# Decoder trunk on one core: 48 of the 64 chunk products of the recurrent output projection moved into the last three rounds as plain fp32

## What is computed

```python
def rwkv7_time_mix(...):
    ...
    y = rwkv7_scan(rh, decay.reshape(B, S, H, N), kh, vh, -kk, kk * ah)
    ...                                   # per-head norm, bonus
    out = ((y + bonus.reshape(B, S, D)) * g).astype(h.dtype) @ w_o
    return out, v_first

x = x + y
x = x + swiglu_ffn(rms_norm(x, ffn_norm[layer]), ffn_w_in[layer], ffn_w_out[layer])
```

## Time and profile before

| | us |
|---|---|
| time, median of 3 runs (1957.79 to 1961.66) | 1959.42 |
| the profiled execution: its own time | 1955.48 |
| the profiled execution: span from first to last instruction | 1953.7 |
| round 3, gated to gated (sixteen projection products) | 52.45 |
| round 4 (sixteen) | 52.93 |
| round 5 (eight) | 52.42 |
| round 6 (none) | 50.61 |
| round 7 (none, and no "after" part) | 35.62 |
| round 8 (none, only the "before" part) to the first `w_o` product | 20.54 |
| first `w_o` product to the end of the first feed-forward tile | 51.28 |

### The profile page before, as it was taken

One profiled execution on the slowest core, in us unless ns is written; L12 is line 12 of the kernel. 1 busy time (PEld: TensorE's weight loads), 2 busy tenths in 40 slices (PEclk: granted clock), 3 DMA queues, 4 the chain that ended last, 5 costly groups with the idle time before them and its releaser, 6 DMA issues.

```text
span 1953.7 us, 35112 instructions
## 1 busy us (share of the span) xinstructions
PE 1853.1 (95%) x15020; PEld 1425.4 (73%) x15020; DVE 946.0 (48%) x1593; ACT 781.8 (40%) x1326; POOL 205.1 (10%) x174
## 2 busy tenths in 40 slices
PE   8978999987889999999999999999999799999999
PEld 3745666655658888888887877777777588888887
DVE  6624555555535444443355545545554564444422
ACT  4333343333324222222345656566656442222211
POOL 0032333323210000000011111111111000000000
PEclk9989999998879999999999999999999899999999
DMA  3281010100213333333332222222222133333332
GB/s 119 78 262 35 17 30 29 29 27 5 70 37 94 100 95 99 95 105 91 95 99 85 69 73 76 85 68 76 76 69 72 30 101 97 97 97 97 97 97 97
DMA packets 57539, 154.95 MB, mean 79 GB/s; under 512 B 5591, under 2 KB 22535, under 8 KB 57384
## 3 DMA queue, kind: packets, MB, share of 16 engines
q1 hardware_dynamic: 57288, 152.63, 25.8%
q10 hardware_dynamic: 96, 0.07, 0.0%
HBM read 150.51 MB, written 11.61 MB: 83 GB/s over the span
## 4 chain that ended last, share of the span: by engine, by line
PE 86%; ACT 4%; DVE 4%; issue 3%; SPq 1%; DMA 1%; POOL 0%; ACTq 0%; DVEq 0%
PE bank L500 84%; PE bank L503 2%; ACT f L1415 2%; ACT f L1428 1%; SPq L459 1%; DMA f<-stream 1%; DVE f L1628 1%; SPq L442 1%; DVE f L1636 0%; ACT f L1402 0%; ACT f L1174 0%; DVE f L1511 0%; DVE f L1514 0%; DVE r L1488 0%; DVE f L1595 0%
## 5 line engine op out<-in xcount | busy, mean ns | idle before, releaser
L500 PE MATMUL bank<-r 128*128 128x512 f32 x5616 | 1304.8, 392 | 7.0 <-DVE r L1915 3.7
L500 PEld LDWEIGHTS bank<-r 128*128 128x128 f32 x5616 | 1051.0, 188 | 241.9 <-issue 18.0
L500 PE MATMUL bank<-f 64*64 64x64 f32 (+3 forms) x8940 | 503.8, 258 | 70.0 <-DVE f L1605 12.4
L500 PEld LDWEIGHTS bank<-f 64*64 64x64 f32 (+2 forms) x8940 | 321.1, 143 | 234.2 <-issue 120.9
L1488 DVE TENSOR_TENSOR r<-f,r 128x1024 fp32r<-128x1024 f32 x230 | 283.0, 1231 | 390.4 <-ACT r L1102 390.4
L1102 ACT ACTIVATE r<-f 128x1024 fp32r<-128x1024 f32 x230 | 240.7, 1047 | 153.4 <-PE bank L500 138.2
L2066 POOL TENSOR_TENSOR r<-f,r 128x512 fp32r<-128x512 f32 x48 | 62.2, 1297 | 886.1 <-ACT r L1393 886.1
L1372 ACT ACTIVATE r<-f 128x512 fp32r<-128x512 f32 x44 | 27.8, 632 | 218.1 <-DVE f L1808 218.1
L1839 DVE TENSOR_TENSOR f<-bank,f 128x512 f32<-128x512 f32 x72 | 56.0, 777 | 87.6 <-PE bank L500 84.6
L503 PEld LDWEIGHTS bank<-f 128*128 128x128 f32 x464 | 54.3, 143 | 48.6 <-ACT f L1428 26.9
L503 PE MATMUL bank<-f 128*128 128x128 f32 x464 | 70.4, 282 | 20.3 <-ACT f L1428 14.3
(11 more groups left out here) (110 smaller groups left out, 974.6 us busy)
## 6 DMA issues: line engine op xcount, KB each, us to landing
f<-stream SPq DMA_DIRECT2D x247, 512.0 KB, 3.6
bias_copies<-bias_rows SPq DMA_DIRECT2D x3, 3072.0 KB, 25.5
f<-xT SPq DMA_DIRECT2D x16, 256.0 KB, 4.1
f<-lora_out SPq DMA_DIRECT2D x16, 128.0 KB, 3.9
f<-bias_copies SPq DMA_DIRECT2D x16, 128.0 KB, 3.3
f<-bias_copies SPq DMA_DIRECT2D x32, 64.0 KB, 3.0
outT<-f SPq DMA_DIRECT2D x8, 256.0 KB, 4.5
f<-const SPq DMA_DIRECT2D x1, 576.0 KB, 3.9
```

Source lines behind the costliest of these rows:

```text
L500: return nc.tensor.matmul(out, lhsT, rhs, start=start, stop=stop, skip_group_check=True)
```

## The change

Of the 64 (tile, chunk) products of the output projection, 48 are computed while the rounds still run, as plain fp32 products like those of `project`, in the places where `project` has nothing left to do: 15 in round 6, 16 in round 7 and 17 in round 8. They take the tiles in turn: five chunks of tiles 0, 1 and 2, six of tiles 3 and 4, seven of tiles 5, 6 and 7. All sum up in bank 6, tile 6 in bank 5. DVE adds each partial tile to x (`partial(m)`), and PE waits for that before it begins the next tile in the bank. The other sixteen products are plain fp32 too, from two panels of their own (`wo_last`), in banks 2, 3 and 4: six stand right behind the last round, ten behind the last pair's output. The first two feed-forward tiles are computed together, chunk by chunk (`first_pair`), between and behind the last of these products, and `norm_sum` follows both. The six `w_o` panels of the early products are no longer split, nor are the time mixer's outputs, and so `output_high`, `output_low` and the splits of `w_o` panels go. In all three `residual` calls the scaled copy (a `tensor_scalar` on DVE) goes: ACT rounds straight from x with the gain as scale, and DVE forms the low part with one `scalar_tensor_tensor`. x is loaded again from HBM, and `wo_last` with it, in SP's round 6 rather than behind the rounds.

```diff
+EARLY_WO = [(m, c) for m, n in enumerate((5, 5, 5, 6, 6, 7, 7, 7)) for c in range(n)]
+LAST_WO = [(m, c) for m, n in enumerate((5, 5, 5, 6, 6, 7, 7, 7)) for c in range(n, KC)]
+        EARLY_AT = {NHP - 2: 0, NHP - 1: 15, NHP: 31, NHP + 1: 48}
+        def early_bank(m):
+            return banks[5 if m == 6 else 6]
+        def bank_of(t):
+            if T_WO0 <= t < T_IN0:
+                return banks[2 + (t - T_WO0) % 3]
+            return banks[5 if t == T_IN0 + 2 else t % 2]
...
+                if k == NHP - 2:
+                    sp.wait_ge(s["dense"], PANEL_AT[PAN_PROJ + proj_of_value(NHP - 1)])
+                    for c in range(KC):
+                        sp.dma_start(xk(c), xT[c * P:(c + 1) * P, :]).then_inc(s["x_again"], 16)
+                    sp.dma_start(f(O_WHI + LAST_AT, 1024), wo_last[0]).then_inc(s["wo_last"], 16)
+                    sp.dma_start(f(O_WLO + LAST_AT, 1024), wo_last[1]).then_inc(s["wo_last"], 16)
+                    panel(PAN_WO0 + RAW)
...
+            def output_early(k, step):
+                at = EARLY_AT[k] + step
+                last_step = (k, step) == (NHP, 2 * KC - 1)
+                for i in range(at, min(at + 1 + last_step, EARLY_AT[k + 1])):
+                    m, c = EARLY_WO[i]
+                    p, col = divmod(i, 8)
...
+                    elif c == 0 and m != 6:
+                        pe.wait_ge(s["wo_part"], min(m, 6))
...
+                    last = mm(early_bank(m)[:, :], raw(PAN_WO0 + p, col), f(O_A + c * S), c == 0, tile_end)
...
+            for m in range(3):
+                output_last(m, range(5, KC - 1))
             for b in range(2):
                 pe.wait_ge(s[f"bank{b}_free"], len(SIDE_TURN[b]))
             for m in range(KC):
-                product(T_WO0 + m, 8 * (PAN_WO0 + m), lambda c: r(O_A + (KC + c) * S), lambda c: r(O_A + c * S),
-                        KC, "yo_lo" if m == 0 else None)
+                if m >= 3:
+                    pe.wait_ge(freed(T_WO0 + m - 3), (T_WO0 + m - 3) // 2 + 1)
+                    output_last(m, [c for n, c in LAST_WO if n == m])
+                else:
+                    output_last(m, [KC - 1])
+                if m >= 4:
+                    first_pair(m - 4)
+            for c in range(4, KC):
+                first_pair(c)
+            norm_sum(1)
...
+            def partial(m):
...
+                    dve.wait_ge(s["wo_ps"], m + 1)
+                TT(xk(m), early_bank(m)[:, :], xk(m), ALU.add).then_inc(s["wo_part"], 1)
...
-                    TT(r(O_XG + (KC + m) * S), f(base + i % 2 * S), rf(O_XG + m * S), ALU.subtract)\
+                    STT(r(O_XG + (KC + m) * S), xk(m), vec(gain, m), rf(O_XG + m * S), ALU.mult, ALU.subtract)\
                         .then_inc(s["xg_lo"], 1)
                 for m in range(KC):
-                    split_low(p_of(t0 + m) + LEAD)
+                    if n:
+                        split_low(p_of(t0 + m) + LEAD)
+                    elif m in (0, 2):
+                        split_low(PAN_IN0 + m // 2)
...
-                    TS(f(base + i % 2 * S), xk(m), vec(gain, m), None, ALU.mult).then_inc(s["xg_t"], 1)
```

More of the change, by code:

```diff
@@ L505, in product @@
             def product(t, q0, rhs_hi, rhs_lo, chunks, gate=None, gate0=0, part=None):
-                if t >= 2 and part in (None, 0):
+                if t >= 2 and part in (None, 0) and not T_IN0 <= t <= T_IN0 + 2:
                     pe.wait_ge(freed(t), t // 2)
-                bank = banks[t % 2]
+                bank = bank_of(t)
                 for j in range(chunks) if part is None else [part]:
@@ L932, in _, with output_last, first_pair @@
                 project(k, 15)
+            def output_last(m, chunks):
+                for c in chunks:
+                    p, col = divmod(LAST_WO.index((m, c)), 8)
+                    w = (O_WLO if p else O_WHI) + LAST_AT + col * P
+                    last = mm(bank_of(T_WO0 + m)[:, :], f(w, P), f(O_A + c * S),
+                              (m, c - 1) not in LAST_WO, c == KC - 1)
+                    if c == KC - 1:
+                        last.then_inc(s["dense"], 1)
+            def first_pair(c):
+                for t in (T_IN0, T_IN0 + 1):
+                    product(t, 8 * (PAN_IN0 + t - T_IN0), lambda c: r(O_XG + c * S), lambda c: r(O_XG + (KC + c) * S),
+                            KC, "xg_lo", 0, c)
+            pe.wait_ge(s["wo_last"], 32)
+            pe.wait_ge(s["y0_sb"], 2 * NHP)
+            side_read(pe, 0, "g", NHP - 2)
+            for m in range(3):
+                output_last(m, range(5, KC - 1))
             for b in range(2):
@@ L2060, in _ @@
                     b_units(k + 1)
-                for hp in YO_AT.get(k, []):
-                    output_low(hp)
             for n in range(6 * NHP):
```

113 lines of the change are left out of this document (70 added, 43 removed).

## The result

The changed kernel took **1942.08 us** (median of 4 runs, 1937.35 to 1944.45) against 1959.98 for the kernel before on the same chip (4 runs, 1957.79 to 1961.66): a ratio of 0.9906, 95% interval 0.9884 to 0.9928. Faster was forecast, with 1946.4 and a range of 1936 to 1956. The profiled execution after took 1937.35 us (span 1935.5, mean granted clock 0.992); that of before 1955.48.

What follows compares the result with a forecast made beforehand. It took a chain of waits, mostly on PE, as the bound, with PE never waiting from 612.52 on. Summed steps start the fourth feed-forward tile at 610.8 instead of 623.8: 13.0 us off the median 1959.42 gives 1946.4, range 1936 to 1956.

Steps and rivals of the forecast that it cites:

- rounds 6 and 7: Last rounds with 15 and 16 early products: forecast to grow by 4.7 us (to 55.3) and by 7.5 us.
- From the profile to the median: Whole kernel: gain of 13.0 us taken from the median 1959.42 (1946.4), not from the profiled 1955.48 (1942.5).
- Round 5 and the start of round 6: Round 5 untouched, its clock fall at 449.42 stays: 0; slow start of round 6 up to the first walk: +1.1 us.
- The wait for `partial(0)`: Round 6, sixth product: PE stands still 1.4 to 1.6 us until DVE's add is done; 1.5 taken.
- Round 7: Sixteen products, no preparation of a next pair: +7.5 us, bounds +4 to +9.5.
- The wait for `partial(4)`: Round 7, between `readout` and the output gate: PE waits for DVE's add, +1.8 us.
- Round 8 and the clock: Round 8 up to `variance`: products add 2.7 us, full clock instead of half gives back 1.7; +1.0, bounds -1 to +3.
- the third rival: Pauses let the clock fall in round 8; two half-clock stretches make it slower, 1966 us; chance of slower 0.07.
- The pair of tiles: Last ten products and first two feed-forward tiles: DVE paces at 2.05 us a tile; 22.1 us, bounds 20.5 to 24.
- The wait ahead of the fourth tile: Behind `norm_sum`: fourth feed-forward tile waits about 1.0 us for DVE to empty its bank, bounds 0 to 2.
- The first rival: Products free in the rounds: rounds 6 and 7 grow by 2 us each, gain 21, 1938 us; chance 0.14.
- the second: Rival: feed-forward pairs fail to overlap with DVE, gain about 4 us, 1955; chance 0.13, shared with dearer waits or one slow stretch.

Runs made afterwards that it cites:

- the changed kernel's second run: The changed kernel once more, unaltered, on another chip: 1942.0 us against 1955.23 for the kernel before, ratio 0.9933.
- the first experiment on the waits: Changed kernel with DVE's `partial(0)` taken up ahead of `bonus_terms` and `partial(4)` ahead of `transitions`: 1938.23 us, ratio 0.9913 to the kernel before.
- the better version: Changed kernel with both partial adds earlier, and feed-forward panel splits and the second tile's copy-out reordered: 1936.89 us, in a second set 1935.99.

## Why the prediction was right, and where its sizes were off

The mechanism was the one forecast: rounds 6 and 7 pay for the products (+11.3 found, +12.2 forecast), round 8 pays little, and the end of the output projection and the first two feed-forward tiles, solid PE work now, more than give it back. The sizes, step by step:

**From the profile to the median.** The prediction put 3.9 us on top of its own sum of 1942.5, since the profiled execution lay that far below the median of the runs shown. The changed kernel's median is 1942.1, the sum without that. Three more sets of runs of before, 7, 7 and 11 of them, have medians of 1955.23, 1955.36 and 1953.76: the profiled 1955.48 was the ordinary run, and the first runs lay high. Against the set on its own chip the changed kernel's second run gains 13.2 us, as forecast; the first comparison has 17.9 and the two profiles 18.1. That the forecast of the gain came so near is partly luck, because the steps below differ from it by up to 2.6 us each.

**Round 5 and the start of round 6 (0 and +1.1 forecast, -2.6 and 0 found).** The prediction held that the fall of the clock at 449.42 would stay because it comes of untouched code. In the profile after it isn't there; round 5 is shorter by 2.57, and from `gated` to the first walk round 6 is as fast as round 4. The step that failed is that a fall seen in one profile is a property of the code. Of the twelve profiles of this case, eight have a fall of 10.2 us that begins between 447 and 451, one has a shorter one at 428.9, and three have none there (one of those three is the kernel with round 5 filled). Where round 6 began with the fall and had the wait, it took 55.80 against 55.3 forecast (one profile); without the fall, 53.68 to 54.45 (four). The term was right and its condition was not certain.

**The wait for `partial(0)`, 1.5 forecast.** The row says 1.41, and taking it away gave 1.27 back.

**Round 7 (+7.5 forecast, +8.2 found).** DVE's timeline of round 7 after, the first three `x_masked`, answers to the earlier trace rows:

```profile
506.60 1.41 DVE L1695 TENSOR_TENSOR f<-bank,f 64x512 f32<-64x512 f32 x2 [0.34 <-PE bank L517]
...
512.21 1.41 DVE L1695 TENSOR_TENSOR f<-bank,f 64x512 f32<-64x512 f32 x2 [1.60 <-PE bank L517]
...
518.26 1.41 DVE L1695 TENSOR_TENSOR f<-bank,f 64x512 f32<-64x512 f32 x2 [1.60 <-PE bank L517]
```

The first begins 506.60 - 505.57 = 1.03 after `gated` (1.2 forecast), and from the second to the third it takes 518.26 - 512.21 = 6.05, the duration that the prediction took over from round 4. The other levels differ by place (5.61 from the first to the second and from the third to the fourth), and all of them together grew by 4.1 (4.6 forecast). The two products behind the solution lie in PE's wait there, as forecast: from DVE's copy of the solution to its first copy of the transitions it is 0.15 more than before. The wait for `partial(4)` is 1.56 (1.8 forecast), and without it the stretch from `readout` to `gated` is 1.63 shorter. What the prediction did not have is a wait inside `readout`'s own products. PE's timeline, then DVE's:

```profile
542.06 0.93 PE L517 MATMUL bank<-f 64*64 64x64 f32 x48 [1.36 <-issue]
```

```profile
540.07 1.69 DVE L1719 TENSOR_TENSOR f<-bank,f 64x192 f32<-64x192 f32 x4 [2.56 <-PE bank L517]
543.05 0.84 DVE L1730 TENSOR_TENSOR f<-bank,f 128x256 f32<-128x256 f32 x2 [1.30 <-PE bank L517]
```

PE stands still for 1.36 us between two small products with no semaphore between them (`issue` says that the profile shows nothing it waited for), so DVE's `readout` starts 2.98 us behind its first copy of the transitions. Before, PE ran through here without a wait, and it was 538.42 - 536.70 = 1.72: +1.26. The profile names nobody who ended this wait. Waits of this kind stand in the kernel before too, at other places (one of 1.26 ahead of 495.06, one of 1.17 ahead of 444.19), and each profile of the kernels here whose round 7 holds 16 more products has one at this place, of 1.01 to 1.36. Between 536 and 548 the only packets that any queue moved are two of the instruction queue, 16 KB each. In all eleven profiles with the added products one of these packets lands 1.4 to 1.6 us before this wait ends, and the wait goes with the time that the packet took: 1.01 to 1.08 us where that was 0.87 to 0.96, and 1.24 to 1.36 where it was 1.12 to 1.26. Products of one column leave it in place (1.24). That fits a wait for code and not one for work, but the kernel before has such a packet there too, landing at 537.87, and no wait; no run tested it. The sum is -1.85 + 4.1 + 0.15 + 1.26 + 4.5 = +8.2.

**Round 8 and the clock (+1.0 forecast, +0.46 found).** The clock was 1.00 up to `variance` and on. In the five profiles that have the wait for `partial(4)`, full products in all three rounds and the changed kernel's order, three have a fall that begins right behind that wait, two of 3.4 us and one of 6.8, and in none does half clock come back in round 8 for the 26 us that the third rival needed. In the three profiles without that wait (the first experiment on the waits, and the better version twice) nothing falls there.

**The pair of tiles (22.1 forecast, 20.90 found).** This is the step with the wrong bound. The prediction gave DVE 2.05 us for each tile and so made it the slower engine. One turn of it in the profile after, from add to add, with the last low part behind:

```profile
584.83 0.69 DVE L1872 TENSOR_TENSOR f<-bank,f 128x512 f32<-128x512 f32 x1
585.43 0.74 DVE L1860 SCALAR_TENSOR_TENSOR r<-f,r 128x512 fp32r<-128x512 f32 x1
586.09 0.69 DVE L1566 TENSOR_TENSOR f<-f 128x512 f32<-128x512 f32 x1
586.69 0.68 DVE L1872 TENSOR_TENSOR f<-bank,f 128x512 f32<-128x512 f32 x1
...
596.00 0.75 DVE L1860 SCALAR_TENSOR_TENSOR r<-f,r 128x512 fp32r<-128x512 f32 x1
```

The durations are those forecast (0.69, 0.74, 0.69), but the next instruction starts 0.6 us, 0.66 and 0.6 after the last: 586.69 - 584.83 = 1.86 a turn. With 2.05 six turns are 1.1 us longer, which is nearly all of the miss (the forecast's own terms, 19.75 + 6 x 0.227 + 0.87, add up to 22.0 rather than 22.1). At 1.86 PE is the bound, as the windows say (20.86 of 20.90), and the lower bound of the prediction (PE alone, 20.5) was the better value; the better version, which has DVE's splits done ahead of the first add, comes to within 0.1 of it. With the scaled copy a turn is 2.33, and DVE is the bound again: the edit in `residual` is what moved it to PE.

**The wait ahead of the fourth tile (1.0 forecast, 0.71 found).** DVE splits a panel from 603.77 and takes the second tile out at 604.92, in the order that the prediction read from the earlier trace rows; in the other order the wait is gone.

```profile
603.77 1.23 DVE L1555 TENSOR_TENSOR r<-f,r 128x1024 fp32r<-128x1024 f32 x1 [2.20 <-ACT r L1174]
604.92 0.68 DVE L1893 TENSOR_TENSOR f<-bank,f 128x512 f32<-128x512 f32 x1
```

The first rival, free products, fell with the products added to the kernel before (+10.1 us); the second, no overlap, with the pair undone. What is left open is why the clock falls at the end of round 5 in most executions and not in all: the same code stands before it in nearly all of these kernels, and one filled round is too little to say what holds it.

## What to carry to other kernels

Work put into an engine's pauses is not free because the engine looks idle there: price it by a pair of like stretches of the same trace, one with and one without the work (here 27 us of PE time cost 11.9), and look for the gain where the work was taken from, as an earlier start of a stretch in which the engine never waits. For the pace of an engine measure from start to start of a repeated group; a sum of durations, with a little taken off for overlap, said 2.05 where the group takes 1.86, and named the wrong bound. Where a moved step hands its result on through a second engine, take it up there one step earlier: two changes of place in DVE's order gave 2.9 us by rows, and with three more behind the rounds the kernel came to about 1936 us.

## What the runs showed of the hardware

The granted clock isn't a fixed part of a kernel's time. The same program fell to half clock at 374.30, 428.90 and 548.40 in one execution, for 3.40 us each, and at none of these places in another; the rounds with a fall were together 6 us longer, more than any single size that the prediction missed (the two executions as a whole lie 4.8 us apart). Taking PE time away gave little: 48 products cut to one column brought 1.3 us, with 54.6 us at half clock between 450 and 577 in its profile, where the profile after has none. And adding idle products to the kernel before raised its mean clock from 0.981 to 0.991.
